# A two-layer decoder step on one core: where the shared expert's down product and the embedding's projection run

## The reference, cut to what matters

```python
x = layer_norm(ALPHA * x + mixer(x))
scores = sigmoid(x @ w_router)             # 64 experts, 8 groups
...                                        # best 4 groups, best 8 experts, gates
def expert_step(acc, ew):
    wg, wu, wd, gcol = ew                  # 1024x256, 1024x256, 256x1024
    h = silu(xt @ wg) * (xt @ wu)
    return acc + gcol[:, None] * (h @ wd), None
shared = (silu(xt @ w_sg) * (xt @ w_su)) @ w_sd
x = layer_norm(ALPHA * x + acc + shared)
gate = sigmoid(x @ w_ple_gate)
x = x + gate * (p[i] @ w_ple_proj)         # p[i]: 288 x 256
```

## Time and profile before

| what | value |
|---|---|
| median of 3 runs (lowest to highest) | 1651.85 us (1649.35 to 1655.16) |
| the profiled execution | 1652.17 us, its span 1650.4 us |
| TensorE busy (matmul) | 1568.3 us, 95% |
| VectorE, ScalarE, GpSimd busy | 33%, 21%, 9% |
| the chain that ended last | TensorE 83%, DMA 10%, VectorE 3% |
| bytes read from HBM | 526 MB |
| DMA engines' busy share, slices inside the loops | 0.9 or more, but for one slice a layer (0.8) |

### The profile page before, as it was taken

One profiled execution on the slowest core, in us unless ns is written; L12 is line 12 of the kernel. 1 busy time (PEld: TensorE's weight loads), 2 busy tenths in 40 slices (PEclk: granted clock), 3 DMA queues, 4 the chain that ended last, 5 costly groups with the idle time before them and its releaser, 6 DMA issues.

```text
span 1650.4 us, 22440 instructions
## 1 busy us (share of the span) xinstructions
PE 1568.3 (95%) x8258; PEld 791.6 (48%) x8258; DVE 540.2 (33%) x1328; ACT 342.1 (21%) x702; POOL 144.8 (9%) x222
## 2 busy tenths in 40 slices
PE   8998999999999999999999999999999999999988
PEld 5774544443444434456565655454443444444334
DVE  2156522222222222441434434462222222222235
ACT  2111121221222211221222221112221211221122
POOL 0330000000000000000111111010000000000000
PEclk9988999999999999999999999999999999999999
DMA  9643799999989999963567576579999998999970
GB/s 303 247 125 143 289 400 420 420 421 420 414 360 421 420 421 417 353 231 108 178 235 244 197 269 223 211 279 381 421 420 420 420 419 358 420 421 421 418 275 30
DMA packets 121321, 536.14 MB, mean 325 GB/s; under 512 B 17848, under 2 KB 29368, under 8 KB 73503
## 3 DMA queue, kind: packets, MB, share of 16 engines
q1 hardware_dynamic: 98023, 470.35, 71.5%
q0 software_dynamic: 21360, 61.64, 10.3%
q10 hardware_dynamic: 1872, 3.22, 0.6%
HBM read 526.15 MB, written 23.87 MB: 333 GB/s over the span
## 4 chain that ended last, share of the span: by engine, by line
PE 83%; DMA 10%; DVE 3%; issue 2%; ACT 1%; SPq 1%; POOL 0%; ACTq 0%; DVEq 0%
PE ps L1268 22%; PE ps L1140 13%; PE ps L1118 12%; PE ps L1295 11%; DMA weights<-in_w_exp_up 10%; PE ps L1244 6%; PE ps L1261 3%; PE ps L1240 2%; PE ps L1279 2%; PE ps L1288 1%; PE ps L1135 1%; PE ps L1034 1%; PE ps L1315 1%; PE ps L1012 1%; PE ps L1025 1%
## 5 line engine op out<-in xcount | busy, mean ns | idle before, releaser
L1268 PE MATMUL ps<-weights,x_feat 128*64 128x512 f32 x1856 | 409.3, 593 | 27.7 <-DMA weights<-in_w_exp_up 14.6
L1268 PEld LDWEIGHTS ps<-weights,x_feat 128*64 128x64 f32 x1856 | 136.6, 137 | 294.7 <-issue 294.7
L1295 PE MATMUL ps<-weights,arena 128*64 128x512 f32 x992 | 226.5, 598 | 0.9 <-ACT arena L1481 0.9
L1118 PE MATMUL ps<-x_feat,weights 128*128 128x288 f32 x832 | 210.6, 411 | 1.1 <-issue 1.1
L1118 PEld LDWEIGHTS ps<-x_feat,weights 128*128 128x128 f32 x832 | 160.2, 194 | 45.5 <-issue 4.0
L2140 DVE CAST split<-state 128x1024 fp32r<-128x1024 f32 (+1 forms) x66 | 44.8, 678 | 325.0 <-ACT state L1481 325.0
L2137 DVE SCALAR_TENSOR_TENSOR arena<-arena,ps 128x256 f32<-128x256 f32 x64 | 30.8, 480 | 357.0 <-ACT arena L1710 357.0
L2461 POOL DMA_INDIRECT arena<-x_rows,arena x64 | 63.5, 992 | 886.7 <-DVE arena L2130 841.0
L1481 ACT ACTIVATE state<-ps 128x512 f32<-128x512 f32 x132 | 78.8, 597 | 287.5 <-PE ps L1295 261.0
L1140 PE MATMUL ps<-weights,x_feat 128*128 128x512 f32 x288 | 126.7, 594 | 6.0 <-DVE x_feat L2330 3.0
L1295 PEld LDWEIGHTS ps<-weights,arena 128*64 128x64 f32 x992 | 65.7, 136 | 132.3 <-issue 130.9
(11 more groups left out here) (289 smaller groups left out, 1294.4 us busy)
## 6 DMA issues: line engine op xcount, KB each, us to landing
weights<-in_w_exp_gate SPq DMA_DIRECT2D x124, 1024.0 KB, 14.7
weights<-in_w_exp_up SPq DMA_DIRECT2D x124, 1024.0 KB, 18.1
weights<-in_w_exp_down SPq DMA_DIRECT2D x124, 1024.0 KB, 16.6
weights<-in_w_in_c SPq DMA_DIRECT2D x24, 1024.0 KB, 9.0
arena<-in_state_ret POOLq DMA_DIRECT2D x20, 512.0 KB, 5.6
out_ret_sample<-arena POOLq DMA_DIRECT2D x20, 512.0 KB, 6.7
weights<-in_w_in_a SPq DMA_DIRECT2D x8, 1024.0 KB, 10.3
weights<-in_w_ple_gate SPq DMA_DIRECT2D x8, 1024.0 KB, 18.1
```

The lines of the kernel that those rows point to most:

```text
L1118: last = pe.matmul(ps[:, 0:T], lhs(c), XT[:, c, :], start=(c == 0), stop=(c == n - 1))
L1268: last = pe.matmul(ps[64 * s:64 * s + 64, :], XGT[u][:, c, 64 * s:64 * s + 64], rhs, start=(c == 0), stop=(c == KC - 1))
L1295: last = pe.matmul(ps[64 * s:64 * s + 64, :], HT[u][:, c, 64 * s:64 * s + 64], wd[s][:, c, 512 * n:512 * n + 512], start=(c == 0), stop=(c ...
```

## The change

It does six things, in both layers.

1. The home pair stands at place 8 (the ninth) and not at 16.
2. The shared expert's down products leave the stretch ahead of the loop. They run behind the down products of pair 20 (chunk 0) and 21 (chunks 1 and 2), and the sum banks are opened by pair 1's `sums` (`start=opening`).
3. The projections leave the stretch behind the loop. They run at the ends of pairs 22 (chunk 2), 23 (chunk 0) and 24 (chunk 1), in banks 2 and 1, and ScalarE copies them at once (`keep_projection`); the next pair's `turn_rows` waits for that.
4. Both weights (1 MB and 1 MB) are loaded into the second half of the home pair's space, in SyncE's queue behind panel pair 9 and as soon as the home pair's gate and up product is done. `PP` overlays the first half. For the products to stand in code of their own, pairs 20 to 25 are written out (`LATE`).
5. `cum` comes ahead of `shared(1)`, and `shared(3)` behind the lists and the flag. SyncE waits for the first two gathers before it issues panel 5.
6. The tables and the scale and shift of the sampled chunk (32 rows) go from VectorE to GpSimd, ahead of its clearing of the gather tiles and of the stores of `x_rows`.

```diff
-HOME = 16
+HOME = 8
...
+SHARED_AT = {20: (0,), 21: (1, 2)}
+PROJECT_AT = {22: 2, 23: 0, 24: 1}
+PROJECTED = {22: 1, 23: 3, 24: 5}
+LATE = range(10, 13)
 
 LOOP_USES = {0: 2 * PAIRS, 1: 3 * PAIRS - 3, 2: 2 * PAIRS - 1}
...
         HOME_UP = [AR[:, TOP + PW * k:TOP + PW * k + PW] for k in range(2)]
         PP = AR[:, TOP:TOP + 3 * D].rearrange("p (j n) -> p j n", j=3)
+        PROJ = HOME_UP[1][:, 0:2048].rearrange("p (f n) -> p f n", f=2)
+        WSD = HOME_UP[1][:, 2048:3072], HOME_UP[1][:, 3072:4096]
         a = Cut(AR[:, 0:EARLY], EARLY)
...
-                            for f in range(2):
-                                sp.dma_start(WSD[f], A["w_sh_down"][l, P * f:P * f + P, :]).then_inc(sem("shared_down_in"), 16)
                         if 3 * pr + k == 5:
                             for q in range(2):
                                 if q:
 
-                                    sp.wait_ge(sem("x_affine", l, 1), 3)
+                                    sp.wait_ge(sem("x_affine", l, 1), 2)
+                                    sp.wait_ge(sem("sample_affine"), l + 1)
                                 sp.dma_start(HOME_DOWN[q], A["w_exp_down"][l, E - 2 + q].rearrange("(p c) n -> p (c n)", c=2)
                                              ).then_inc(sem("home_in"), 16)
+                            for u in range(2):
+                                sp.wait_ge(sem("gathered", u), 8 * PAIRS * l + 16)
                         wait_slot(n0 + 3 * pr + k)
                         if pr == 0 and k < 2:
...
+
+                sp.wait_ge(bank_full[0], base[0] + uses(0, HOME, 1))
+                for f in range(2):
+                    sp.dma_start(WSD[f], A["w_sh_down"][l, P * f:P * f + P, :]).then_inc(sem("late_in"), 16)
+                for f in range(2):
+                    sp.dma_start(PROJ[:, f, :], A["w_ple_proj"][l, P * f:P * f + P, :]).then_inc(sem("late_in"), 16)
                 with sp.Fori(HOME // 2 + 1, PAIRS // 2 - 1) as it:
...
-                tp = lambda w: w.rearrange("(f p) n -> p f n", p=P)
-                panel((f"proj{l}",), lambda dst: [
-                    (dst[:, 1024 * f:1024 * f + 1024], tp(A["w_ple_proj"][l])[:, f, :]) for f in range(2)])
...
-                shared(1)
                 pe.wait_ge(sem("chosen"), l + 1)
...
 
...
+                def shared_down(j):
+
+                    o, r = CH[j]
+                    pe.wait_ge(sem("late_in"), 64 * (l + 1))
+                    for f in range(2):
+                        emptied(pe, (f"sh{l}", 2 + f))
+                    for c in range(2):
+                        if j == 2:
+                            for q in range(4):
+                                pe.matmul(PS[TS * q:TS * q + TS, 7, 0:256], HSf[:, c, o:o + r], WSD[c][:, 256 * q:256 * q + 256],
+                                          start=False, stop=False, skip_group_check=True)
+                            continue
+                        for n in range(2):
+                            pe.matmul(bank((f"sum{l}", j, n)), HSf[:, c, o:o + r], WSD[c][:, 512 * n:512 * n + 512],
+                                      start=False, stop=False, skip_group_check=True)
+
+                def project(j, pr):
+
+                    o, r = CH[j]
+                    pe.wait_ge(sem("late_in"), 64 * (l + 1))
+                    emptied(pe, (f"pT{l}",))
+                    emptied(pe, (f"cum{l}",))
+                    if j == 2:
+                        for c in range(2):
+                            for q in range(4):
+                                cols = PROJ[:, c, :].rearrange("p (n q x) -> p n q x", n=2, q=4)[:, :, q, :]
+                                last = pe.matmul(PS[TS * q:TS * q + TS, 2, 0:256].rearrange("p (n x) -> p n x", n=2),
+                                                 PT[:, c, o:o + r], cols, start=(c == 0), stop=(c == 1))
+                        last.then_inc(sem("projected"), 1)
+                        return
+                    for n in range(2):
+                        if n:
+                            pe.wait_ge(bank_free[1], base[1] + uses(1, pr, 3))
+                        for c in range(2):
+                            last = pe.matmul(PS[:, 2 - n, :], PT[:, c, o:o + r], PROJ[:, c, 512 * n:512 * n + 512],
+                                             start=(c == 0), stop=(c == 1))
+                        last.then_inc(sem("projected"), 1)
...
-                pe.wait_ge(sem("shared_down_in"), 32 * (l + 1))
-                for f in range(2):
-                    emptied(pe, (f"sh{l}", 2 + f))
-                for j, (o, r) in enumerate(CH):
-                    for n in range(2 if j < 2 else 1):
-                        ps = begin((f"sum{l}", j, n))
-                        for c in range(2):
...
+                shared(3)
                 pe.wait_ge(sem("flag_ready"), l + 1)
                 go = pe.value_load(flagi[0:1, 0:1], min_val=0, max_val=1)
                 pe.wait_ge(sem("gathered", 0), 8 * PAIRS * l + 16)
...
+                        if isinstance(pr, int) and pr - 1 in PROJECTED:
+                            pe.wait_ge(sem("projection_kept"), 5 * l + PROJECTED[pr - 1])
...
-                                sums(0, n, v)
+                                if opening:
+                                    begin((f"sum{l}", 0, n))
+                                sums(0, n, v, start=opening)
                         if not tail:
...
+                    two_pairs(it, True)
+                for it in LATE:
+                    two_pairs(it)
+                with pe.Fori(LATE.stop, PAIRS // 2 - 1) as it:
                     two_pairs(it, True)
...
                     tok((f"pg{l}", j, n), lambda c: XT[:, c, o:o + r], lambda c: w[:, c, :], r, KC)
 
-                project(0)
-                project(1)
                 transpose_x(f"xTc{l}", 0, (sem("x_ln2", l), 1))
                 have_xt(f"xTc{l}", (0,))
                 gate_logits(0, 0)
                 transpose_x(f"xTc{l}", 2, (sem("x_ln2", l), 2))
                 gate_logits(0, 1)
-                project(2)
...
+                def keep_projection(j, count):
+
+                    if j == 2:
+                        act.wait_ge(sem("projected"), 5 * l + count)
+                        for q in range(4):
...
+                    for n in range(2):
+                        act.wait_ge(sem("projected"), 5 * l + count - 1 + n)
+                        copy(PP[:, j, 512 * n:512 * n + 512], PS[:, 2 - n, :]).then_inc(sem("projection_kept"), 1)
...
-            for j in range(3):
+            for j in range(2):
                 affine(l, 1, j)
-
-            st.run(dve.memset(MSK, 0.0))
-            st.run(dve.memset(POS, -1.0))
-            for j in range(3):
-                for k, t in ((3, tok_even), (4, tok_odd)):
-                    st.run(TSc(TAB[:, j, :, k], iota[:, 0:E], 0.0, t[:, j:j + 1], ALU.mult, ALU.add))
-            st.run(dve.memset(TAB[:, :, :, 5], -FAR))
-            st.after
+            dve.wait_ge(sem("tables_set"), l + 1)
             emptied(dve, (f"scores{l}",))
             dve.wait_ge(sem("rbias_in"), 16 * (l + 1))
...
-            shared(1)
+            shared(0)
+            dve.wait_ge(sem("sample_affine"), l + 1)
...
+            shared(1)
...
+            st.run(pool.memset(MSK, 0.0))
+            st.run(pool.memset(POS, -1.0))
+            st.run(pool.memset(TAB[:, :, :, 5], -FAR))
+            for j in range(3):
+                for k, t in ((3, tok_even), (4, tok_odd)):
+                    st.run(pool.tensor_scalar(TAB[:, j, :, k], iota[:, 0:E], 0.0, t[:, j:j + 1], ALU.mult, ALU.add))
+            st.after.nop().then_inc(sem("tables_set"), 1)
+            pool.wait_ge(sem("ln_in", l, 1), 32)
+            for q in range(2):
+                full(pool, (f"xTb{l}", 2, q))
+            x = X[0:TS, 2, :]
+            st.run(pool.tensor_tensor(x, x, norm_place(l, 1)[0][0:TS, :], ALU.mult))
+            st.after
+            st.tell(pool.tensor_tensor(x, x, norm_place(l, 1)[1][0:TS, :], ALU.add), sem("sample_affine"))
             for u in range(2):
                 st.run(pool.memset(XG[u], 0.0))
...
             for j, (o, r) in enumerate(CH):
-                pool.wait_ge(sem("x_affine", l, 1), j + 1)
+                if j == 2:
+                    pool.wait_ge(sem("sample_affine"), l + 1)
+                else:
+                    pool.wait_ge(sem("x_affine", l, 1), j + 1)
```

90 lines of the change are left out of this document (42 added, 48 removed), and 3 rows, old and new, of the table FIXED_BANKS.

## The result

The change made the kernel slower. The median is 1663.81 us (1660.44 to 1664.71, 5 runs) against 1651.85 us; the ratio on record is 1.0063, with a 95% interval of 1.0050 to 1.0077. The profiled execution took 1660.44 us (span 1658.6) against 1652.17: 8.3 us of difference for the traces to explain, the rest of the median's 12 is spread between executions.

What follows compares the result with a forecast made beforehand. Two close limits bound the loop: TensorE at 14.58 us a pair, transfers at 15.85. Terms -1.7 and -5.3 (layer 0), -1.8 and -8.0 (layer 1) sum to -16.8 us from 1652.17: 1635 us, range 1627 to 1645.

Steps and rivals of the forecast that it cites:

- ends 2.6 us earlier: Ahead of the loop: without tables and a third of affine, VectorE's selection starts at 166.5 and ends at 173.4.
- rival 1: Ahead of the loop: GpSimd and VectorE shut each other out, or gathers are late; one 1639 to 1642, both 1646; chance 0.15.
- Same code and same pattern in both layers, so layer 0's numbers serve for both.: Ahead of the loop: layer 0's gain of 5.9 us was taken for layer 1 too.
- -5.9: Ahead of the loop, each layer: pair 0 starts at 189.4 and not at 195.34 in layer 0.
- +4.2: Loop, each layer: of 5.9 us won ahead of it, 4.2 go back through transfer waits and new TensorE work.
- harmless slack: Loop, at pair 24: a DMA gap only uses 1.9 us of the transfers' slack at the end; one gap under 4 us.
- -5.3: Behind layer 0's loop: projections go, norm is next late; transposes 4.4 us earlier, project(2) 0.9 us less.
- -8.0: Behind layer 1's loop: the gain of layer 0, and 2.75 us of TensorE idle time now covered by the norm.
- Rival 3: Loop: the new work is paid in full, 11.7 us a layer more, 1658.5 us, slower; chance 0.05.
- Rivals 2 and 4: Transfers do not limit, 1626 us (0.08); no change, home pair's gap unfilled and GpSimd or gathers late, 1647 to 1656 (0.08).
- The gap at the home pair: Loop: the new loads, 5.0 us of DMA, fill the transfers' pause while the home pair frees no slot for 21.6 us.
- signs of being wrong: GpSimd's row instructions over 3 us each, gathers landing later than 6 us, or waits for weights behind pair 24.

Runs made afterwards that it cites:

- experiment 1: Changed kernel with the tables and the affine of the sample rows back on VectorE: 1663.06 us, ratio 1.0074 to the kernel before.
- Experiment 2: Changed kernel with shared product 1 in bank 7 in place of 5: 1654.46 us, ratio 1.0017 to the kernel before.
- experiment 5: Changed kernel with the five products spread over pairs 14, 17, 20, 22 and 26: 1654.89 us, ratio 1.0022 to the kernel before.
- experiment 3: Changed kernel with the products put in at pairs 12 to 16 in place of 20 to 24: 1661.31 us, ratio 1.0059 to the kernel before.
- experiment 6: Changed kernel without the overflow branch on TensorE, which these inputs never take: 1658.80 us, ratio 1.0047 to the kernel before.
- experiment 4: Changed kernel with six extra unused products on TensorE behind the last sums of each layer's loop: 1659.37 us, ratio 1.0045 to the kernel before.

## Why the prediction was wrong

It said 1635 us; the kernel took 1663.8. The place of the waits and the time that the gather takes to land were about right; pair 0, the last pair and all behind it came later than forecast. What failed:

**VectorE's selection "ends 2.6 us earlier".** It ended 0.5 us earlier by experiment 1. The first half of rival 1 held: the two engines shut each other out. I had given it 0.15, since no row showed the two side by side. This was 2 us a layer, and 1639 would have been the sum. The Trainium skill (SBUF — State Buffer, section "SBUF: two separate sides") says that of a two-input VectorE instruction and a GpSimd instruction that reads SBUF, the one that starts first holds the shared ports to its end and the other waits. For GpSimd's two-input instructions the trace agrees: 3.26 us in place of 1.23 beside GpSimd's 2.84, with the ends where that order puts them. For its tables the trace shows one direction only: they took 3.89 us in place of 1.94, while no affine of VectorE beside them took over 1.23. The landing of the gather, the other half of the rival, was 4.4 us (4.2 in layer 1) and not late.

**"Same code and same pattern in both layers, so layer 0's numbers serve for both."** This step failed most: -5.9 was forecast for layer 1, +1.6 came, and another 1.4 at pair 0's first products. The rotation of banks is not the same in both layers, while the new table names fixed ones. The order of the groups shows only the bank's number, and I read it for layer 0. Experiment 2 gave 7.6 us back for the one digit.

**The loop, "+4.2".** It was +6.7 and +7.9. Pair 20 came 296.2 us behind pair 0 and not 295.0; from there to the last pair 177.4 us and not 176.3, since the new work is 16.6 us and not 15.9. In layer 1 it was 297.0, with pair 0's 1.4 us at the lower clock in it, and 177.4. The mechanism (waits at 16 to 20, none behind) was seen as forecast. Its worth was not: I counted pauses of the transfers as harmless slack, as TensorE no longer waited. In experiment 5 the 3.3 us of lost transfers were gone and the loop of layer 0 was 3.0 us shorter; in experiment 3 the pauses only stood elsewhere, and it was as long as before. So here a pause cost about its length. By that the loop had 3.0 and 3.3 us more to give (the 4.7 of experiment 5 in layer 1 less pair 0's 1.4).

**"-5.3" behind loop 0 and "-8.0" behind loop 1.** +0.1 and -5.8 came. What I had put down as pure cost, the projections on the chain, had two covers that I did not price. They lay over the time that goes with the skipped branch (3.1 us on the chain in layer 0, experiment 6), and they kept TensorE's clock up while the norm ran (2.7 us in layer 0: 0.8 at the transposes and 1.9 at the logits; 2.5 in layer 1, experiment 4). With these, -5.3 becomes +0.5 and -8.0 becomes -5.5, against +0.1 and -5.8. I had seen the 2.75 us of the earlier trace rows in layer 1 and written that the norm covers all of that now. It did there. In layer 0 a stall of the same look turned up with twice the length.

**Also not priced**: idle time of TensorE ahead of the masks. `shared(1)` had filled it. In four of nine profiles the clock fell in it, for 2 us in layer 0.

Rival 3 ended on the right side, slower, for the wrong reason: the new work was not paid in full. Rivals 2 and 4 did not occur. The gap at the home pair closed as forecast (a DMA share of 1.01 in every window from 195 to 490). Of the signs of being wrong that I had named, one came: GpSimd's second row instruction took 3.21 us in both layers. Between the forecast of -16.8 and the +8.3 of the profiles lie 25 us: 9.0 ahead of the loops, 6.2 in them, 7.6 behind them, and 2.2 in the two stretches that the change does not touch.

What stays open: the 12 us of the medians against 8.3 of the profiles (the fall of the clock ahead of layer 0's lists, which the changed kernel's profile doesn't have and four of nine have, would be 0.9 us of it on the mean), and why the stall behind the branch varies in layer 0: none is seen in the kernel before, 1.8 us in run 3, 5.5 in the changed kernel.

## What to carry to other kernels

Work that is moved away had neighbours: list what it covered (idle time in which a clock falls, a stall behind a branch, an engine's wait) and price each as if the cover were gone. Where a ring of transfers is nearly the bound, put extra compute in small pieces at the points where the lead is just used up, and count a pause of the transfers as lost until a run shows that it is not. Fixed buffer numbers must be read for every repetition of the code, not for the first.

## What the runs showed of the hardware

- TensorE's granted clock fell to 0.50 (1.2 GHz) while it idled 5.53 us (0.64 in 685 to 690, 0.50 in 690 to 695), and to 0.64 behind 2.48 us idle (1610 to 1615). Behind shorter waits it fell in some places (0.66 in 1115 to 1120, behind 1.41 and 1.06 us) and not in others (1.66 us idle at 177.33, product 1 at 4.15 us behind it). What runs next pays: 4.15 us of products became 6.9 to 7.0.
- GpSimd's instruction over 32 x 1024 with two inputs took 2.34 us where it began ahead of VectorE's (layer 1, 1079.90) and 2.84 to 3.21 where it began behind one. VectorE's of 1.23 us took 3.25 to 3.29 beside them.
- Behind a skipped branch TensorE stood for nothing that the profile names, for up to 5.5 us; the length differed between programs with the same branch, and without the branch it was gone.
